# Second mixing output in eight units of three passes, with the block inversion and the first inverse's expansion placed earlier

## The chip, the cores and the metric

The kernel runs on one core of one Trainium2 chip. The metric is the device time of one execution in microseconds (us). The profile is one execution on that core; its times count from the first instruction.

## What is computed

Two transformer-like blocks run over 256 tokens of width 1024, all in float32. The first block (attention, an LRU mixer, two gated feed-forward layers) is not touched. The change lies in the second block, between its input projections and its feed-forward layer:

```python
p = concat([h_ctx, h_lat]) @ w_in               # q k v z, rq rk rv rg, for 512 tokens
o_gdn = rms_norm(o_f + o_b, gdn_norm_g) * silu(z)      # gated delta rule, forward and backward
o_ret = head_group_norm(r_f + r_b, ret_norm_g) * silu(rg)   # retention, forward and backward
y = concat([o_gdn, o_ret])                      # 256 latent tokens x 1024
x = x + g1 * (y @ w_out)                        # "second mixing output"
x = x + g2 * swiglu(modulate(rms_norm(x), sh2, sc2), w_ffn_in, w_ffn_out)
```

The delta rule needs, for each tile of 128 tokens, head and direction, the inverse of a unit triangular matrix. The kernel inverts its 16x16 diagonal blocks by substitution, row after row, for all tiles at once, and joins them to the 128x128 inverse in three levels of products.

## The kernel before

Each engine has its own program, written out by hand; semaphores order them. There is no scheduler. Weights stream from memory in chunks of 2 MB into `ring`, which has three slots; `stream_order` is the order of the chunks, and the load of chunk i waits on SyncE's queue until chunk i-3 is counted in `chunk_used`. The last chunks before the feed-forward layer are `win` (eight), `wo2` (two halves of w_out) and `ada` 9 to 11 (modulation), then `up2`.

**Split products.** Most products are made of two reduced-precision parts. For a unit of weights (128x1024) ScalarE copies the high part into `parts` (`high_parts`, L311; an input of the product as well, L334), VectorE subtracts it to get the low part (`low_parts`, L315 and L346), and TensorE makes three passes, low by high, high by high, high by low. `parts` holds three units, so unit n+3 can be copied only when TensorE has counted unit n in `parts_used`. `SplitProjection` does this for a product whose input is turned tiles: a unit is 12 matmuls of 512 columns; of the last three units it makes the first 128 tokens' rows first. `high_ahead` and `low_ahead` split a unit's weights before its input exists.

**The stretch in question**, in order:

- The projections end with `w_rq` and `w_rg` (four units each). `rotated` applies the rotary embedding to `w_rq`'s result on VectorE and `gated` the gate of `w_rg`.
- VectorE inverts the 16x16 blocks (`invert_rows`): row i is one multiply and one reduction for each direction, of i*i elements. Rows 1 to 8 come before `gated`, rows 9 to 11 in retention's step 0 and rows 12 to 15 in its step 1. The result goes through memory (`inverses_out`, then 16 small DMAs, `inverse_rows_in`), and `expand` spreads it over the tile `X`.
- Retention runs in four steps over both directions. In steps 0 to 2 TensorE makes the state's update (`rdS`) and VectorE adds it (`update_state`, L1771 and L1774); in steps 2 and 3 TensorE makes the scores (`rqk`), the product with the state and, after VectorE's mask (L1828), the product with the values (`ro`), which `output_part` evicts (L1757 to L1762).
- The delta rule runs in four steps. In each TensorE turns `X` (L2306), ScalarE copies it (`XT`), three levels of `Y` and `Z` products alternate with VectorE (L1891 to L1912), then come `wT`, `vnew`, the state's update and, in steps 2 and 3, `o`, evicted by `output_part` again. `beside` is a table of small VectorE tasks put beside these levels.
- Then `y` is turned tile by tile, and `heads_projection` multiplies it by w_out in full float32, from `ring` directly: retention's half first, the delta rule's half after its norm. One matmul of 128x512 in float32 stands in the trace as two records.
- `beside_norm` makes modulation chunks 10 and 11 beside the residual and the norm, and `up_ffn2` starts (L407).

`parts` lies over columns 13312 to 20991 of the scratch memory `arena`, so the tiles of retention and the delta rule that lie there exclude split weights.

## Time and profile before

| | |
|---|---|
| median of 3 runs | 1436.04 us (1434.91 to 1438.17) |
| the profiled execution's own time | 1437.29 us |
| its span, first to last instruction | 1435.5 us |
| TensorE busy | 1341.1 us, 93% |
| VectorE busy | 908.0 us, 63% |
| ScalarE busy | 673.0 us, 47% |
| mean granted TensorE clock | 0.968 |

The busy share is an average over all stages. The stretch of the change runs from about 1012 us (the end of VectorE's work for `w_rq`'s weights) to 1238 us (the first matmul of the feed-forward layer), 226 us; there TensorE does wait.

### The profile page before, as it was taken

How to read it: one execution, taken by the hardware profiler on the slowest of the kernel's cores; microseconds unless marked ns; L12 is line 12 of the kernel's file. 1: busy time of each engine (PE TensorE's matmuls, PEld its weight loads, DVE VectorE, ACT ScalarE, POOL GpSimd, SP SyncE). 2: the span in 40 equal slices, each digit the busy share in tenths (PEclk: the TensorE clock that was granted, in tenths of full speed). 3: DMA queues.
4: the chain of work that ended last, by engine and by line, in shares of the span. 5: the costliest groups of instructions: out<-in, count | busy, mean ns of one | idle time of the engine just before them, and what ended most of it. 6: DMA issues, size and time to landing. Idle time of an engine off the chain costs nothing.

```text
span 1435.5 us, 19067 instructions
## 1 busy us (share of the span) xinstructions
PE 1341.1 (93%) x7776; PEld 1141.9 (80%) x7776; DVE 908.0 (63%) x1394; ACT 673.0 (47%) x1043; POOL 65.5 (5%) x105
## 2 busy tenths in 40 slices
PE   7999999888999999899999989999879989899997
PEld 5899978777888878868888767868779884588885
DVE  4444443356888758577889767558776541566665
ACT  4444544345676645755666653334401110455453
POOL 1000000000000000000000000210121100000000
PEclk9999999998999999999999999999979998999999
DMA  9643334546454566356545472125410003554451
GB/s 361 252 175 120 118 135 159 208 152 240 162 191 176 184 226 250 116 196 241 195 177 183 177 271 93 59 86 186 159 16 1 1 1 117 222 189 176 176 196 69
DMA packets 31525, 230.16 MB, mean 160 GB/s; under 512 B 11168, under 2 KB 14624, under 8 KB 18512
## 3 DMA queue, kind: packets, MB, share of 16 engines
q1 hardware_dynamic: 25712, 218.27, 41.9%
q10 hardware_dynamic: 4720, 7.02, 1.3%
q0 software_dynamic: 1008, 3.67, 0.6%
q8 instruction: 61, 1.00, 0.3%
q14 instruction: 24, 0.20, 0.0%
HBM read 225.50 MB, written 3.44 MB: 159 GB/s over the span
## 4 chain that ended last, share of the span: by engine, by line
PE 80%; DVE 11%; ACT 5%; issue 2%; DMA 1%; POOL 0%; POOLq 0%; ACTq 0%; DVEq 0%; SPq 0%
PE ps L407 17%; PE ps L197 14%; PE ps L579 13%; PE ps L458 10%; PE ps L411 9%; PE ps L546 5%; PE ps L449 5%; PE ps L518 4%; DVE parts L315 2%; PE ps L490 2%; ACT parts L311 1%; DVE arena L1463 1%; ACT arena L1086 1%; DMA ring<-in_W 1%; PE ps L1987 1%
## 5 line engine op out<-in xcount | busy, mean ns | idle before, releaser
L315 DVE TENSOR_TENSOR parts<-ring,parts 128x1024 fp32r<-128x1024 f32 x346 | 422.7, 1226 | 290.9 <-ACT parts L311 222.9
L311 ACT ACTIVATE parts<-ring 128x1024 fp32r<-128x1024 f32 x346 | 365.1, 1057 | 303.6 <-PE ps L411 104.8
L407 PE MATMUL ps<-hall,parts 128*128 128x512 f32 x1120 | 397.9, 399 | 12.3 <-DVE hall L271 6.5
L411 PE MATMUL ps<-hall,parts 128*128 128x256 f32 x1120 | 316.2, 282 | 0.0
L407 PEld LDWEIGHTS ps<-hall,parts 128*128 128x128 f32 x1120 | 212.4, 190 | 64.5 <-issue 12.0
L579 PE MATMUL ps<-parts 128*128 128x512 f32 x1032 | 241.9, 394 | 8.5 <-DVE parts L346 7.5
L579 PEld LDWEIGHTS ps<-parts 128*128 128x128 f32 x1032 | 194.3, 190 | 53.7 <-DVE parts L346 12.3
L411 PEld LDWEIGHTS ps<-hall,parts 128*128 128x128 f32 x1120 | 214.3, 191 | 0.0
L197 PE MATMUL ps<-arena 128*128 128x128 f32 (+2 forms) x1238 | 171.9, 300 | 22.7 <-DMA arena<-in_rel_bias 7.3
L197 PEld LDWEIGHTS ps<-arena 128*128 128x128 f32 (+1 forms) x1238 | 160.5, 202 | 32.0 <-issue 8.6
L458 PE MATMUL ps<-hall,parts 128*128 128x256 f32 x1152 | 140.4, 284 | 0.7 <-ACT arena L1050 0.7
L458 PEld LDWEIGHTS ps<-hall,parts 128*128 128x128 f32 x1152 | 138.7, 192 | 1.1 <-ACT arena L1050 1.1
L1463 DVE SCALAR_TENSOR_TENSOR arena<-arena,par 128x255 f32<-128x255 f32 (+1 forms) x192 | 80.1, 480 | 18.8 <-ACT arena L1086 18.0
L546 PE MATMUL ps<-parts,hall 128*128 128x512 f32 x336 | 82.6, 402 | 2.1 <-DVE parts L315 2.1
L546 PEld LDWEIGHTS ps<-parts,hall 128*128 128x128 f32 x336 | 63.2, 190 | 17.9 <-DVE parts L315 3.0
L449 PE MATMUL ps<-parts,hall 128*128 128x512 f32 x288 | 68.6, 398 | 4.5 <-DVE hall L266 2.5
L449 PEld LDWEIGHTS ps<-parts,hall 128*128 128x128 f32 x288 | 54.7, 192 | 17.6 <-ACT arena L1050 3.3
L518 PE MATMUL ps<-hall,parts 128*128 128x512 f32 (+1 forms) x288 | 60.8, 374 | 5.2 <-issue 2.8
L518 PEld LDWEIGHTS ps<-hall,parts 128*128 128x128 f32 x288 | 50.5, 200 | 14.4 <-issue 5.8
L287 POOL TENSOR_SCALAR smallp<-small 128x1 f32<-128x1 f32 x24 | 5.5, 228 | 1056.7 <-ACT arena L629 646.2
L1086 ACT ACTIVATE arena<-arena,par 128x256 f32<-128x256 f32 x96 | 49.6, 587 | 4.0 <-DVE arena L390 4.0
L490 PE MATMUL ps<-hall,parts 128*128 128x256 f32 x384 | 47.4, 285 | 1.5 <-DVE hall L266 1.3
(216 smaller groups left out, 1095.2 us busy)
## 6 DMA issues: line engine op xcount, KB each, us to landing
ring<-in_W SPq DMA_DIRECT2D x100, 2048.0 KB, 8.3
arena<-distance_tables SPq DMA_DIRECT2D x8, 384.0 KB, 7.5
gains<-in_gains POOLq DMA_DIRECT2D x5, 512.0 KB, 7.4
ring<-in_W SPq DMA_DIRECT2D x4, 512.0 KB, 9.1
arena<-in_gate_w ACTq DMA_DIRECT2D x1, 2048.0 KB, 10.8
matrices<-arena ACTq DMA_DIRECT2D x8, 256.0 KB, 2.8
x<-in_x SPq DMA_DIRECT2D x1, 1024.0 KB, 6.3
gates<-in_ada_gate_b POOLq DMA_DIRECT2D x2, 512.0 KB, 6.4
```

What stands on the lines that cost most here:

```text
L197: return nc.tensor.matmul(o, l, r, start=start, stop=stop)
L311: return nc.scalar.activation(unit_weights(n, 0, weights), weights, ACT.Copy)
L315: return nc.vector.tensor_tensor(unit_weights(n, 1, weights), weights, unit_weights(n, 0, weights), ALU.subtract)
L407: last = nc.tensor.matmul(ps[:, b, :].rearrange("p (a b) -> p a b", a=2), w[:, 0, :], hparts[:, :, k, :], start=k == 0, stop=False)
L411: last = nc.tensor.matmul(ps[:, b, 0:S], w[:, 1, :], hparts[:, 0, k, :], start=False, stop=k == KT - 1)
L449: last = nc.tensor.matmul(ps[:, banks[t], :], hparts[:, x_part, k, t * P:(t + 1) * P], parts[:, u % NPARTS, w_part, w0:w0 + 512], start=k ...
L458: last = nc.tensor.matmul(ps[:, banks[n // 2], (n % 2) * S:(n % 2 + 1) * S], parts[:, u % NPARTS, w_part, k * P:(k + 1) * P], hparts[:, x_ ...
L490: last = nc.tensor.matmul(ps[:, 4 + 2 * (i % 2) + n // 2, (n % 2) * S:(n % 2 + 1) * S], parts[:, u % NPARTS, w_part, k * P:(k + 1) * P], h ...
L518: last = nc.tensor.matmul(o, parts[:, u % NPARTS, w_part, k * P:(k + 1) * P], h, start=k == 0 and x_part == 1, stop=k == KT - 1 and w_part ...
L546: last = nc.tensor.matmul(ps[:, b, :], hall[:, t // TT, x_part, k, t % TT * P:(t % TT + 1) * P], parts[:, u % NPARTS, w_part, w0:w0 + 512] ...
L579: last = nc.tensor.matmul(ps[:, 2 * t + half, :], parts[:, n % NPARTS, x_part, D + t * P:D + (t + 1) * P], parts[:, n % NPARTS, w_part, w0 ...
L1463: last = v.scalar_tensor_tensor(dst, src, pcol("ffn_conv_w", (layer * 3 + tap) * 48 + ft), dst, ALU.mult, ALU.add)
```

## The change

1. `invert_rows` moves. Rows 1 to 5 go ahead of the low part of `w_rg`'s first unit, rows 6 to 8 ahead of the second, rows 9 and 10 ahead of the third, and rows 11 to 15 behind the second rotation. Retention's loop holds none. `gated` goes ahead of the masks of retention's decay. The inversion's tile no longer shares memory with the rotation's scratch tile, which moves into `parts`' input columns, and `rotated` takes its operands as 2x2 heads.
2. `expand(0)` goes from behind retention into its last step, ahead of that step's evictions (it waits for the same DMAs), and TensorE turns `X` at the delta rule's step 0 without waiting for retention's outputs; its first `Y` product waits for them.
3. The second mixing output becomes `p_mix2`, a `SplitProjection` of eight units. Units 0 and 1 are split ahead, by ScalarE in the delta rule's step 2 and by VectorE in step 3; retention's half of `y` is turned and copied in step 3; unit 2 waits for the last `o`, since the delta rule's last tiles lie in its buffer. Modulation 9 goes ahead of unit 0, and its chunk ahead of `wo2` in the stream. Tiles of the delta rule leave `parts`' other two buffers for memory of finished operands (`kdec`, `St`, `ET`, `E`).

```diff
-            + [("win", i, 0) for i in WIN_ORDER] + [("wo2", 1, 0)] + ada[9:10] + [("wo2", 0, 0)] + ada[10:12]
+            + [("win", i, 0) for i in WIN_ORDER] + ada[9:10] + [("wo2", 1, 0), ("wo2", 0, 0)] + ada[10:12]
...
+        p_mix2 = SplitProjection(4, [("wo2", 1, 0), ("wo2", 0, 0)], region(2048, KT, S), KT, lambda e, kk: e.wait_ge(S_("yT_out"), kk // 2 + 1))
...
-        later_tiles = [region(16384 + 512 * i, H4, P) for i in range(9)]
-        rkdec, rPm, rSt, St = (later_tiles[2 * i:2 * i + 2] for i in range(4))
-        kdec, ET = rkdec, rPm
-        E = [later_tiles[8], tmpr]
+        later_tiles = [region(16384 + 512 * i, H4, P) for i in range(6)]
+        rkdec, rPm, rSt = (later_tiles[2 * i:2 * i + 2] for i in range(3))
+        kdec = [region(11264 + 512 * d, H4, P) for d in range(2)]
+        St = [kT[:, :, P * d:P * (d + 1)] for d in range(2)]
+        ET = [vT[:, :, P * d:P * (d + 1)] for d in range(2)]
+        E = rET
...
+                if step == 2:
+                    for ahead_unit in (0, 1):
+                        high_ahead(act, p_mix2.first + ahead_unit)
...
+                if step == STEPS - 1:
+                    y_out(0)
+                    y_out(1)
+                    high_parts(act, p_mix2.first + 2)
+            act.wait_ge(S_("o"), 4)
+            high_parts(act, p_mix2.first + 3)
+            ada_rows(ADA_MIDDLE)
             for i, t in enumerate((1, 0)):
                 act.wait_ge(S_("o_out"), 7 + i)
                 head_squares(0, t)
+            high_parts(act, p_mix2.first + 4)
+            for ahead_unit in (4, 5):
+                high_ahead(act, p_mix2.first + ahead_unit)
+            y_out(2)
+            y_out(3)
+            p_mix2.scalar(act)
...
+            invert_rows(1, 6)
+            low_parts(dve, u0 + 29)
+            invert_rows(6, 9)
+            low_parts(dve, u0 + 30)
+            invert_rows(9, 11)
             low_parts(dve, u0 + 31)
             w_rq.done(dve)
             rotated(w_rq, 0, rq[:, 0, :, :], 0)
             low_parts(dve, u0 + 32)
             rotated(w_rq, 1, rq[:, 1, :, :], TT2 + TT + 1)
+            invert_rows(11, BLK)
...
-                    if step == 0:
-                        invert_rows(9, 12)
-                    if step == 1:
-                        invert_rows(12, BLK)
+                if step == STEPS - 1:
+                    dve.wait_ge(S_("lvl_in"), 16)
+                    dve.wait_ge(S_("inverse_rows_in"), 16 * 2 * NB)
+                    for d in DIRS:
+                        expand(0, d)
...
-                      (2, 0): lambda: delta_gates(0), (2, 2): lambda: delta_gates(1)}
+                      (2, 0): lambda: delta_gates(0), (2, 2): lambda: delta_gates(1),
+                      (3, 0): lambda: low_ahead(dve, p_mix2.first), (3, 1): lambda: low_ahead(dve, p_mix2.first + 1)}
...
+                if step == STEPS - 1:
+                    low_parts(dve, p_mix2.first + 2)
                 if step >= 2:
                     for d in DIRS:
                         dve.wait_ge(S_("o"), later(step, d))
                         output_part(0, step, d, 4 * d, 4 * d + 2)
+            low_parts(dve, p_mix2.first + 3)
...
-            pe.wait_ge(S_("mixed"), 2)
             pe.wait_ge(S_("vnew_out"), 8)
-            y_transposes(4, 5)
-            y_transposes(6, 7)
-            pe.wait_ge(S_("yT_a"), 2)
+            ada(ADA_MIDDLE)
             pe.wait_ge(S_("o_out"), 8)
-            heads_projection(1)
-            ada(ADA_MIDDLE)
+            p_mix2.unit(pe, 0)
             ada_turn(ADA_MIDDLE)
+            for kk in range(1, 4):
+                p_mix2.unit(pe, kk)
             pe.wait_ge(S_("mixed"), 4)
             pe.wait_ge(S_("ada_out"), ADA_MIDDLE + 1)
-            y_transposes(0, 4)
-            y_transposes(2, 6)
-            pe.wait_ge(S_("yT_a"), 3)
-            pe.wait_ge(S_("yT_v"), 1)
-            heads_projection(0)
+            y_transposes(2)
+            y_transposes(3)
+            p_mix2.tensor(pe, 4)
```

VectorE's program from the last unit of `w_rg` on, before: a rotation's end (L1650), the inversion (products L1789 into `row`, reductions L1795), the masks (L1818), the gate (L1654) and retention's first two evictions (L1771).

```order
L1650 TENSOR_TENSOR arena<-arena 128x512
L1810 MEMSET arena 128x512
L1813 MEMSET arena 128x16 x2
...
L1789 TENSOR_TENSOR row<-arena,row 128x64 x2
L1795 TENSOR_REDUCE arena<-row 128x8 x2
L1818 TENSOR_TENSOR arena<-arena,cst 128x4x128 x2
L1654 SCALAR_TENSOR_TENSOR arena<-arena,ps 128x512 x2
L1771 COPY arena<-ps 128x512 x2
L1789 TENSOR_TENSOR row<-arena,row 128x81 x2
L1795 TENSOR_REDUCE arena<-row 128x9 x2
```

The same place of the change (rotation L1669, inversion L1766 and L1772, gate L1673, masks L1844, evictions L1824 and L1827):

```order
L1669 TENSOR_TENSOR arena<-arena 128x512
L1766 TENSOR_TENSOR row<-arena,row 128x121 x2
L1772 TENSOR_REDUCE arena<-row 128x11 x2
...
L1766 TENSOR_TENSOR row<-arena,row 128x225 x2
L1772 TENSOR_REDUCE arena<-row 128x15 x2
L1673 SCALAR_TENSOR_TENSOR arena<-arena,ps 128x512 x2
L1844 TENSOR_TENSOR arena<-arena,cst 128x4x128 x2
L1824 COPY arena<-ps 128x512 x2
L1827 SCALAR_TENSOR_TENSOR arena<-arena,ps 128x128 x8
```

Rows 1 to 10 now stand ahead of the second-last rotation, rows 11 to 15 behind the last, and nothing of the inversion between retention's evictions.

TensorE's program from the delta rule's last step to the norm, before (transposes of `y` L2370, the full float32 product L197 from `ring`, modulation L1987):

```order
L197 MATMUL ps<-row,arena 128x128 x8
L197 MATMUL ps<-arena 128x128 x40
L2370 MATMUL ps<-cst,arena 128x128 x8
L197 MATMUL ps<-ring,arena 128x512 x16
L1987 MATMUL ps<-ring,condT 32x512 x8
L197 MATMUL ps<-sel,row 128x2 x4
L2370 MATMUL ps<-cst,arena 128x128 x8
L197 MATMUL ps<-ring,arena 128x512 x16
L1987 MATMUL ps<-ring,condT 32x512 x16
```

And of the change (transposes L2317, split product L579, modulation L2014):

```order
L197 MATMUL ps<-row,arena 128x128 x8
L2317 MATMUL ps<-cst,arena 128x128 x8
L197 MATMUL ps<-arena 128x128 x40
L2014 MATMUL ps<-ring,condT 32x512 x8
L579 MATMUL ps<-parts 128x512 x12
L197 MATMUL ps<-sel,row 128x2 x4
L579 MATMUL ps<-parts 128x512 x36
L2317 MATMUL ps<-cst,arena 128x128 x8
L579 MATMUL ps<-parts 128x512 x48
```

Eight transposes went ahead of the last step's 40 products, and 32 float32 matmuls became 96 of one pass.

## Rows read from the trace of the kernel before

**Rows 1.** The page: busy time, share of the span and instructions of each engine.
```profile
PE 1341.1 (93%) x7776; PEld 1141.9 (80%) x7776; DVE 908.0 (63%) x1394; ACT 673.0 (47%) x1043; POOL 65.5 (5%) x105
```

**Rows 2.** Stretches: length, busy time (instructions) of each engine, granted clock, DMA.
```profile
1036.40:1045.00 8.60, 8.41 (x48) 8.25 (x48) 5.25 (x14) 0.00 (x0) 4.92 (x5) 0.65 0.01 2
1067.60:1090.00 22.40, 21.88 (x167) 21.30 (x168) 13.56 (x32) 4.83 (x20) 2.08 (x2) 0.88 0.00 1
```

**Rows 3.** Chain that ended last, retention: start, length, what.
```profile
1036.48 3.77 PE ps L197 x16
...
1040.96 0.71 DVE row L1789 x2
...
1053.27 0.61 DVE arena L1828
...
1066.91 0.61 DVE arena L1807
...
1069.60 3.63 PE ps L197 x16
```

**Rows 4.** VectorE alone in stretches: length, busy (instructions), granted clock, DMA.
```profile
1011.96:1026.32 14.36, 8.81 (x13) 1.00 0.41 147
1026.49:1033.64 7.15, 6.48 (x35) 1.00 0.70 246
1040.88:1043.91 3.03, 2.89 (x10) 0.75 0.02 5
1043.91:1045.23 1.32, 1.25 (x5) 1.00 0.00 0
1047.30:1053.27 5.97, 5.73 (x18) 0.95 0.00 0
```

**Rows 5.** VectorE in order of time; in brackets idle before, and its releaser.
```profile
1030.70 1.72 DVE L1789 TENSOR_TENSOR row<-arena,row 128x49 f32<-128x49 f32 x2
...
1035.10 1.29 DVE L1654 SCALAR_TENSOR_TENSOR arena<-arena,ps 128x512 f32<-128x512 f32 x2
```

**Rows 6.** GpSimd in order of time.
```profile
1030.32 2.04 POOL L959 TENSOR_TENSOR arena<-arena 128x512 f32<-128x512 f32 x2 [20.07 <-PE ps L546]
```

**Rows 7.** TensorE in order of time, the delta rule's end.
```profile
1180.45 1.04 PE L2370 MATMUL ps<-cst,arena 128*128 128x128 f32 x8
...
1204.07 1.05 PE L197 MATMUL ps<-sel,row 128*128 128x2 f32 x8 [0.72 <-ACT row L1025]
```

**Rows 8.** Chain that ended last, delta rule's last step to the feed-forward layer.
```profile
1160.42 19.31 PE ps L197 x168
...
1182.43 1.14 DVE arena L1762 x4
...
1185.88 15.61 PE ps L197 x32
...
1207.53 16.73 PE ps L197 x32
...
1224.42 8.89 DMA ring<-in_W
...
1238.22 0.76 PE ps L407
```

**Rows 9.** Chain that ended last, first block's second mixing output (eight units).
```profile
609.89 16.82 PE ps L579 x60
626.74 1.06 ACT parts L311
...
628.14 1.23 DVE parts L315
...
629.75 5.75 PE ps L579 x24
```

**Rows 10.** Chain that ended last, first block's end to the second's projections.
```profile
842.84 5.75 PE ps L579 x24
...
858.97 24.79 PE ps L518 x96
```

More of the change, by code:

```diff
@@ L1736, in _, with invert_rows @@
                 normalized("qn", t)
+            def invert_rows(first, end):
+                if first == 1:
+                    dve.wait_ge(S_("blocks_in"), 16 * 2 * NB)
+                for i in range(first, end):
+                    for d in DIRS:
+                        done = slice(BLK - i, BLK) if d else slice(0, i)
+                        r = BLK - 1 - i if d else i
+                        prod = block_tmp[:, d, 0:i * i].rearrange("p (c j) -> p c j", c=i)
+                        last = v.tensor_tensor(prod, inverses[:, d, done, done].rearrange("p j c -> p c j"),
+                                               blocks[:, d, r, done].unsqueeze(1).to_broadcast([P, i, i]), ALU.mult)
+                    link(last)
+                    for d in DIRS:
+                        done = slice(BLK - i, BLK) if d else slice(0, i)
+                        r = BLK - 1 - i if d else i
+                        last = v.tensor_reduce(inverses[:, d, r, done], block_tmp[:, d, 0:i * i].rearrange("p (c j) -> p c j", c=i),
+                                               AX.X, ALU.add, negate=True)
+                    if i < BLK - 1:
+                        link(last)
+                    else:
+                        last.then_inc(S_("inverses"), 1)
+            link(v.memset(inverses[:, :, :, :], 0.0))
+            for d in DIRS:
+                diagonal = inverses[:, d, :, :].rearrange("p i j -> p (i j)")[:, 0:BLK * BLK:BLK + 1]
+                last = v.memset(diagonal, 1.0)
+            link(last)
+            invert_rows(1, 6)
[3 more added lines that the diff above has]
+            invert_rows(9, 11)
             low_parts(dve, u0 + 31)
@@ L1807, in expand @@
                 v.tensor_tensor(X[d].rearrange("p h (b j) -> p h b j", b=NB), rows, mask, ALU.mult).then_inc(S_("X_in"), 1)
-            link(v.memset(inverses[:, :, :, :], 0.0))
-            for d in DIRS:
-                diagonal = inverses[:, d, :, :].rearrange("p i j -> p (i j)")[:, 0:BLK * BLK:BLK + 1]
-                last = v.memset(diagonal, 1.0)
-            link(last)
-            invert_rows(1, 9)
+            for i in range(TT):
+                gated(w_rg, i, rgt, TT2 + TT)
             for d in DIRS:
@@ L1818, in _ @@
                 link(v.tensor_tensor(rET[d], rET[d], bh(cst[:, C_GE if d else C_LE, :]), ALU.mult))
-            for i in range(TT):
-                gated(w_rg, i, rgt, TT2 + TT)
             for step in range(STEPS):
@@ L1878, in _ @@
                     dve.wait_ge(S_("Y_zero"), 3)
-                    dve.wait_ge(S_("lvl_in"), 16)
-                    dve.wait_ge(S_("inverse_rows_in"), 16 * 2 * NB)
-                    for d in DIRS:
-                        expand(step, d)
                 if step:
@@ L2295, in _, with y_transposes @@
                         heads(4 * d + 2, rPm[d], rv[:, TILE_OF[d][step], :, :]).then_inc(S_("ro"), 1)
+            def y_transposes(i):
+                kind, h = int(i < 2), 2 * (i % 2)
+                for n in range(2):
+                    for t in range(TT):
+                        last = nc.tensor.transpose(ps[:, Y_BANK[i], n * S + t * P:n * S + (t + 1) * P], y2[kind][:, t, h + n, :], ident)
+                last.then_inc(S_("yT"), 1)
             for step in range(STEPS):
-                pe.wait_ge(S_("o_out"), 4 + max(step - 2, 0) * 2)
+                if step > 2:
+                    pe.wait_ge(S_("o_out"), 4 + (step - 2) * 2)
                 if step:
@@ L2330, in _ @@
                         last.then_inc(S_("Z"), 1)
+                if step == STEPS - 1:
+                    pe.wait_ge(S_("mixed"), 2)
+                    for d in DIRS:
+                        pe.wait_ge(S_("decay"), 2 * TT2 + 2 + later(step, d))
+                        y_transposes(d)
                 if step:
```

87 lines of the change are left out of this document (26 added, 61 removed).

## The prediction

> **What bounds the kernel now.** I read the page's engine line first: TensorE is busy 93% of the span [rows 1], so a gain has to come from its idle stretches, from stretches at a low clock, or from less TensorE work. Then the chain of work that ended last, for 1000 to 1240 us, and the same stretch engine by engine. Three places stand out.
>
> Retention: from its first product at 1036.48 to the delta rule's first `Y` product at 1069.60 it takes 33.1 us [rows 3], with TensorE at a granted clock of 0.65 of full speed in the first 8.6 us [rows 2]. The chain there goes through VectorE: inversion rows from 1040.96, more of them until the mask at 1053.27, `expand` at 1066.91 [rows 3]. Rows 9 to 11 take 3.03 + 1.32 = 4.4 us and rows 12 to 15 take 5.97 us [rows 4].
>
> The mixing output: 15.61 and 16.73 us of TensorE [rows 8], 32.3 us for 64 records, about 0.49 us each half a matmul each.
>
> Behind it: the chain goes from TensorE to the DMA of the first feed-forward chunk (8.89 us), which waits for the slot of `wo2`'s second half, and the first matmul starts at 1238.22, 14.0 us after the product's end at 1224.26 [rows 8].
>
> **A, up to retention's start.** VectorE has 14.36 us between 1011.96 and 1026.32, of which 8.81 are busy [rows 4], so 5.5 us are free; the last rotation ends there. Into this go the memsets and rows 1 to 8, 7.15 us [rows 4], of which 1.3 us is one product pair of 1.72 us, whose neighbours in size take 0.34 and 0.43; GpSimd's products ran beside it from 1030.32 to 1032.36 [rows 5, 6]. Without that excess it is 5.8. Rows 9 and 10, 3.03 us [rows 4], at a low-cost reading 2.4. Together 8.2, less 5.5 free: the last rotation ends 2.7 us later, at 1029.0. Behind it rows 11 to 15, 1.32 + 5.97 = 7.3 us [rows 4], to 1036.3. But GpSimd's products still start when `w_rg` is done, near 1030.3, now beside rows 11 to 15; I add half of the 1.3 us seen once, 0.7. The gate takes 1.29 us [rows 5] and ends at 1038.3, against 1036.4: **+1.9 us**, from +1.2 (no collision) to +2.5 (as in the trace).
>
> The GPSIMD Engine Reference of the Trainium skill (section Specifications) says that GpSimd's memory interfaces are shared with VectorE and contended by VectorE instructions with two inputs in that memory. By this rule the products of rows 11 to 15, which have two such inputs, are slowed as the pair of 1.72 us was; that speaks against the change, by at most the +2.5 already in the range.
>
> The low parts of `w_rg`'s four units are done, by the same count, at about 1016.6, 1020.1, 1023.7 and 1026.9. `w_rg` ends where GpSimd's products are released, 1030.3 [rows 6], and a unit takes 2.8 to 2.9 us (half of 5.75, rows 9), so TensorE begins it near 1019 and needs them at 1019.0, 1021.8, 1024.6 and 1027.4. The margin falls from 2.4 to 0.5 us; cost nothing, and each us beyond it moves retention one us.
>
> **B, retention.** Time T counts from its first product. The first two products take 3.77 us at the low clock [rows 3], the next two to T = 6.1 (48 records in 8.41 us, rows 2, less the first 16, make 1.16 for each of four groups of 8). `update_state` follows, four instructions a direction like those of 1.14 us [rows 8], to 7.2. TensorE makes two scores and two products with the state at 0.92 each (19.31 us for 168 records, rows 8, 8 records a product) to 9.8, and two more updates to 11.6; VectorE adds them by 12.9 and evicts step 2 in 3.6 (twice a copy of 0.7 and such four instructions) by 16.5. Masks 1.3 to 17.8, `expand` 1.3 (twice the 0.61 from which the chain goes on) to 19.1, the last evictions 3.6 to 22.7. `X` has been turned and copied beside them, and the first `Y` product starts at about T = 22.8. Before it was 33.1 [rows 3]: **-10.3 us**. 7.6 of it is the inversion rows, less what TensorE now takes in their place; 2.7 is expansion, turning and copy (1066.91 to 1069.60). If half a us more is waited at each hand-over or the low clock lasts to the end, it is -7; if the low clock is shorter than before, -11.5. The inverses' way through memory took 13.6 us at most (the last row ended at 1053.27, and `expand` began at 1066.91 straight behind VectorE's own work, rows 3); from 1037 that is 1050.6, and it is needed at T = 17.8, 1056: hidden.
>
> **C, the delta rule.** In step 3, level 0, VectorE is on the chain into the products at 1160.42 [rows 8], and one unit's low part stands there now: 1.23 us, 1.13 from start to start [rows 9]. At level 1 it has TensorE's four products as cover and costs nothing. Eight transposes, 1.04 us [rows 7], join TensorE's unbroken 168 records. Before, they were hidden under VectorE's last evictions. The low parts of two inputs stand ahead of the last evictions and wait for ScalarE's two copies of `y`; by count they end at the last `o`: +0.1. Sum +2.3. Against that, the delta rule's first 22.4 us ran at a granted clock of 0.88 [rows 2], so a quarter of it at the lower level of 1.2 GHz, after an idle 3.7 us that becomes 1.5: I take back a third of the 2.7 us lost, 0.9. **+1.4 us**, from 0 to +3.
>
> **D, the mixing output.** The nearest rows are the same class in the first block: eight units from 609.89 to 635.50, 25.6 us, with one chain over ScalarE and VectorE of 3.0 us, from 626.74 to 629.75, nearly all beside TensorE's own work [rows 9]. The bare rate is 5.75 us for 24 matmuls, 0.24 each, 23 us for 96. To 25.6 I add modulation 9's turn 1.05 and eight transposes 1.04 [rows 7], and one wait: after the transposes come two copies of `y`, an input's high part and its low part (about 0.5 + 0.4 + 0.35 us beyond the transposes' own end), 1.4 us. That is 29.0 from the last eviction on. Before it was 1183.57 to 1224.26, 40.7 [rows 8], with 2.3 us ahead of it and 6.0 us between the halves. **-11.7 us**. Units 2 to 5 are split beside the squares and the norm, as their buffers come free; the norm's end (by this order about 10 us after the last eviction) lies ahead of unit 3's end (about 14). Bounds: at the bare rate 26, -14.5; with 1 us more of waiting for each of the last four units, -7.7.
>
> FP8 and Floating Point Precision of the Trainium skill (section TensorE Precision Notes) gives true float32 four passes. Three quarters of the 32.3 us would be 24.2 and the gain 1.2 us less than with 23 at the bare rate; The rows, 0.49 us a record and two records a matmul, against three times 0.24, say more; they decide.
>
> **E, behind it.** The slot is released at the first pass of unit 7, with 5 + 18 passes to go, 5.5 us before the end. The DMA of 8.9 us [rows 8] lands 3.4 us after the end, when ScalarE is still at its rows of modulation. What is left is the path without the DMA, as between the first block and the projections, which has the same two modulation chunks and shifted norm: 842.84 + 5.75 = 848.6 to 858.97, 10.4 us [rows 10]. **-3.6 us**, from -2 to -3.7. Nothing else of the feed-forward layer changes.
>
> **Sum.** +1.9 - 10.3 + 1.4 - 11.7 - 3.6 = -22.3 us, against the profiled execution's own 1437.3: 1415.0. That execution lay 1.25 above the median of the runs, so 1413.8, which I put at 1414. The forecast's own range is 1408 to 1420.
>
> **Rivals.**
>
> 1. VectorE is later than counted ahead of retention: a low part of `w_rg` comes late and the inversion collides more. For: margins of 0.5 us, and one pair took four times its size's time. Against: the free 5.5 us are measured. 4 to 6 us back: 1419. Chance 0.12.
> 2. The mixing output follows its buffers: unit n+3 waits for unit n, then 1.06 and 0.34 us of ScalarE, 1.23 and 0.38 of VectorE [rows 9], 3 us against 1.4 for a half unit at the end, and the clock drops in each wait. For: the wait in rows 9. Against: little of it was left on TensorE there, 25.6 us against 23. 4 waits of 1.5 us: 1420. Chance 0.08.
> 3. The gain is larger, since waits close and with them the low clock goes (0.65 and 0.88, rows 2): 1407. Chance 0.07.
> 4. The earlier inversion does nothing for retention, since the inverse's rows come late: VectorE then waits in `expand` ahead of the last evictions. It decides nothing below 5 us more than the 13.6 of before, and one for one beyond. With B gone: 1424. Against: nothing in the way grows. Chance 0.02.
> 5. Slower: TensorE's clock stays at the lower level through the mixing output and the first feed-forward units, since bursts of 2.8 us alternate with waits. 96 passes would take 22.5 us more, which alone gives 1436; two feed-forward units of about 2.8 us more each give 1442. It makes the kernel slower from 25 us of full-speed work at half speed on. For: 8.6 us at 0.65 and 22.4 at 0.88 [rows 2]. Against: 0.24 us a pass in rows 9, with such waits between. Chance 0.07, half of it over 1439.
>
> Forecast 0.64. The range 1407 to 1424 leaves out a part of rivals 3 and 5 and some of the bounds' ends. 0.2%, 2.9 us, is about what a measurement of this kernel can tell from no change: faster 0.93, within 0.03, slower 0.04.
>
> **What the changed profile would show.** Right: retention's first product near 1038.3; no inversion rows in its chain; first `Y` near 1061; step 3 of the delta rule 2 us longer; eight units within 29 us of the last eviction; the next matmul about 10.4 us after them with no DMA in the chain. Wrong: VectorE low parts as releasers of TensorE in `w_rg` (rival 1) or in units 4 to 7 (rival 2), VectorE released by a DMA in `expand` (rival 4), a granted clock near 0.5 over the mixing output (rival 5).

## The result, and the profile after

The changed kernel takes 1408.9 us, the median of 4 runs (1407.0 to 1410.6). The kernel before takes 1436.9 beside it (4 runs, 1434.9 to 1438.2). The ratio is 0.9818, with a 95% interval of 0.9802 to 0.9835: 26 us faster by the ratio, 28 by the two medians. The forecast was 1414, with a range of 1407 to 1424 and an own range of 1408 to 1420. Three single executions in all that follows (two of the kernel before, one of `slot_late`) took 2211 to 4402 us and are left out of every ratio.

The page of the changed kernel, engine lines, which answer to [rows 1]: TensorE has more instructions than before and is busy 20 us less.

```profile
PE 1321.2 (94%) x7808; PEld 1136.3 (81%) x7808; DVE 917.6 (65%) x1409; ACT 683.7 (49%) x1060; POOL 65.4 (5%) x105
```

The stretch of the change in the changed kernel, cut at the same places of the program. Columns as in [rows 2]: start and end, length; busy time and instructions of TensorE's matmuls, its weight loads, VectorE, ScalarE, GpSimd; granted clock; DMA.

```profile
1021.04:1039.91 18.87, 13.77 (x75) 11.62 (x74) 18.32 (x43) 5.83 (x11) 2.13 (x2) 0.92 0.49 187
1039.91:1062.44 22.53, 19.56 (x152) 19.00 (x153) 17.66 (x46) 1.08 (x2) 8.86 (x9) 0.91 0.14 17
1062.44:1099.05 36.61, 34.61 (x297) 33.47 (x297) 26.15 (x60) 4.73 (x20) 5.67 (x5) 1.00 0.01 2
1099.05:1140.55 41.50, 37.53 (x328) 37.00 (x329) 22.90 (x59) 8.95 (x14) 4.08 (x4) 1.00 0.00 1
1140.55:1174.11 33.56, 31.16 (x272) 29.21 (x272) 17.76 (x41) 8.66 (x19) 0.00 (x0) 1.00 0.02 5
1174.11:1200.41 26.30, 24.42 (x116) 19.68 (x120) 14.31 (x26) 10.79 (x28) 1.98 (x2) 1.00 0.59 207
1200.41:1210.26 9.85, 7.47 (x53) 3.36 (x53) 8.03 (x11) 7.22 (x14) 1.49 (x4) 1.00 0.89 336
```

Four of the same stretches of the kernel before, beside [rows 2], which cut them otherwise: retention, the delta rule's first and last step, and the mixing output.

```profile
1036.48:1069.60 33.12, 24.38 (x153) 23.54 (x154) 25.97 (x72) 0.60 (x1) 8.93 (x9) 0.76 0.11 17
1069.60:1107.79 38.19, 36.20 (x296) 35.06 (x296) 26.16 (x60) 5.32 (x21) 5.67 (x5) 0.95 0.01 2
...
1149.30:1183.57 34.27, 32.03 (x256) 31.46 (x256) 14.84 (x37) 6.06 (x16) 0.00 (x0) 0.92 0.00 1
1183.57:1224.26 40.69, 36.48 (x100) 16.06 (x104) 5.89 (x15) 4.58 (x14) 2.79 (x4) 0.87 0.27 104
```

The seven stretches after are, line by line, `w_rg`'s first pass up to retention, retention, the delta rule's first step, its second and third, its last, the mixing output, and what lies behind it up to the feed-forward layer's first matmul. The lengths before and after, by term:

| term of the prediction | before | after | difference | predicted |
|---|---|---|---|---|
| A, up to retention's start | 17.50 | 18.87 | +1.4 | +1.9 |
| B, retention | 33.12 | 22.53 | -10.6 | -10.3 |
| C, delta rule | 113.97 | 111.67 | -2.3 | +1.4 |
| D, mixing output | 40.69 | 26.30 | -14.4 | -11.7 |
| E, behind it | 13.96 | 9.85 | -4.1 | -3.6 |
| sum | 219.24 | 189.22 | -30.0 | -22.3 |

The stretch itself starts 2.1 us later in this execution (1021.04 against 1018.98), by a program that differs up to there in a few of VectorE's instructions and in the order of its last weight chunks; the inversion is not the cause, since TensorE runs into `w_rg`'s first pass without a wait in both. That, and 1.4 us less behind the stretch (197.28 against 195.84), make the difference of the two spans, -29.4.

The chain of work that ended last in the changed kernel, mixing output (start, length, what):

```profile
1172.97 1.14 DVE arena L1815 x4
1174.16 3.02 PE ps L579 x12
1177.17 0.79 PE ps L197 x8
1177.96 8.28 PE ps L579 x36
1186.24 0.45 PE ps L2317 x4
1186.71 1.09 ACT arena L1339 x2
1187.80 0.31 ACT parts L334
1188.13 0.44 DVE parts L346
1188.62 3.03 PE ps L579 x12
1191.67 1.06 ACT parts L311
...
1193.07 1.23 DVE parts L315
...
1194.68 5.73 PE ps L579 x24
1200.41 3.57 PE ps L2014 x32
```

It answers to [rows 8]. The first unit starts 0.05 us after the last `o` (VectorE's L1815 ends at 1174.11), and four units run with only modulation 9's turn between them. Turning `y` and splitting it take 2.38 us (1186.24 to 1188.62, counted as 2.44). Then the chain leaves TensorE for 3.0 us, over a unit's high and low part, as in [rows 9]; TensorE works beside it and is idle 0.33 us. No DMA stands in the chain any more.

### The profile page after: what moved, and what is told of

Same layout as the page of the kernel before. It is cut to its first block, busy times and chain, and to the rows that moved or that the text cites. A ratio compares the mean times of both kernels' runs of the same rounds, so it can differ in the third digit from the quotient of the medians.

```text
span 1406.1 us, 19176 instructions
## 1 busy us (share of the span) xinstructions
PE 1321.2 (94%) x7808; PEld 1136.3 (81%) x7808; DVE 917.6 (65%) x1409; ACT 683.7 (49%) x1060; POOL 65.4 (5%) x105
## 4 chain that ended last, share of the span: by engine, by line
PE 80%; DVE 12%; ACT 5%; issue 2%; DMA 0%; POOL 0%; ACTq 0%; POOLq 0%; DVEq 0%
PE ps L407 17%; PE ps L579 14%; PE ps L197 11%; PE ps L458 10%; PE ps L411 9%; PE ps L546 5%; PE ps L449 5%; PE ps L518 4%; DVE parts L315 3%; PE ps L490 2%; ACT parts L311 1%; DVE arena L1479 1%; PE ps L2014 1%; ACT arena L1087 1%; DVE arena L1815 1%
## 5 line engine op out<-in xcount | busy, mean ns | idle before, releaser
L315 DVE TENSOR_TENSOR parts<-ring,parts 128x1024 fp32r<-128x1024 f32 x354 | 432.5, 1226 | 286.5 <-ACT parts L311 216.5
L311 ACT ACTIVATE parts<-ring 128x1024 fp32r<-128x1024 f32 x354 | 373.5, 1057 | 308.1 <-PE ps L411 105.5
L579 PE MATMUL ps<-parts 128*128 128x512 f32 x1128 | 263.9, 393 | 12.2 <-DVE parts L346 10.0
L579 PEld LDWEIGHTS ps<-parts 128*128 128x128 f32 x1128 | 211.1, 189 | 62.5 <-DVE parts L346 15.8
L197 PE MATMUL ps<-arena 128*128 128x128 f32 (+2 forms) x1238 | 166.4, 294 | 22.9 <-DMA arena<-in_rel_bias 7.1
L197 PEld LDWEIGHTS ps<-arena 128*128 128x128 f32 (+1 forms) x1238 | 154.8, 196 | 32.2 <-issue 13.1
L1479 DVE SCALAR_TENSOR_TENSOR arena<-arena,par 128x255 f32<-128x255 f32 (+1 forms) x192 | 80.0, 480 | 18.7 <-ACT arena L1087 17.9
```

The lines of the kernel that those rows point to most:

```text
L197: return nc.tensor.matmul(o, l, r, start=start, stop=stop)
L311: return nc.scalar.activation(unit_weights(n, 0, weights), weights, ACT.Copy)
L315: return nc.vector.tensor_tensor(unit_weights(n, 1, weights), weights, unit_weights(n, 0, weights), ALU.subtract)
L579: last = nc.tensor.matmul(ps[:, 2 * t + half, :], parts[:, n % NPARTS, x_part, D + t * P:D + (t + 1) * P], parts[:, n % NPARTS, w_part, w0 ...
L1479: last = v.scalar_tensor_tensor(dst, src, pcol("ffn_conv_w", (layer * 3 + tap) * 48 + ft), dst, ALU.mult, ALU.add)
```

## The experiments

All were compared with runs of the kernel before on the same chip; ratios are to it, with a 95% interval, and a difference in us is the difference of two ratios times 1435. They were run in three sets, each on a chip of its own: `inv_only`, `mix_only`, `expand_back` and `before_filled`; `early_f32`, `slot_late`, `gate_first` and `best`; `after_again`, `after_filled` and `early_between`. The change's own 0.9818 is a measurement apart. The same program, run again as `after_again` in the third set, gave 0.9785, 4.7 us less, so a timed difference of under 5 us between sets, or to the change's 0.9818, shows nothing by itself; where it matters, the stretches of the profile decide.

### The two halves of the change apart

`inv_only` is the kernel before with the first two items of the change: `invert_rows` and `gated` moved, `expand(0)` in retention's last step. The mixing output is in float32 from `ring`, as before.

```diff
+            invert_rows(1, 6)
+            low_parts(dve, u0 + 29)
+            invert_rows(6, 9)
...
-                    if step == 0:
-                        invert_rows(9, 12)
-                    if step == 1:
-                        invert_rows(12, BLK)
+                if step == STEPS - 1:
...
+                        expand(0, d)
```

> The kernel before with only the inversion and the first expansion moved, the mixing output still in full float32. Theory (the parts add up): A and B are -9.2 us in the changed profile (+1.4 and -10.6), and about -2 more come with the clock of the delta rule's first step, so 9 to 12 us under before, about 1426; first product of retention to first Y product 22 to 23 us; from the last eviction to the mixing output's end 40 to 41 us as before. Rival (the better clock of the delta rule and of the mixing output belongs to the split product): the delta rule from first Y to last eviction stays at 114 us, and the gain is 8 to 9 us.

`mix_only` is the change with that part put back: `invert_rows`, `gated`, `expand(0)` and the turn of `X` stand as before, the mixing output is in eight units.

> The changed kernel with the inversion rows and the first expansion back at their places of before. Theory: retention takes 33 us again, mixing output 26 to 29 us, 9.9 to 10.4 us behind it; 16 to 19 us under before, about 1419; together with the other part the sum is the change's 28 us. Rival: the two parts need each other (fewer idle stretches, so a full clock into the mixing output), and the mixing output alone takes 28 to 30 us, 13 to 15 us under before.

Measured: `inv_only` 0.9931 (0.9906 to 0.9956), -9.9 us; `mix_only` 0.9898 (0.9881 to 0.9915), -14.6 us. The product of the two is 0.9830, inside the change's interval of 0.9802 to 0.9835 and above that of `after_again` (0.9764 to 0.9806). The stretches of `inv_only`, retention, the start of the delta rule's last step, and the mixing output:

```profile
1034.62:1056.87 22.25, 19.32 (x153) 18.76 (x153) 17.64 (x46) 1.09 (x2) 8.87 (x9) 0.92 0.14 17
1134.96:1146.10 11.14, 10.98 (x72) 10.80 (x73) 4.11 (x11) 2.39 (x4) 0.00 (x0) 0.74 0.01 1
1169.20:1209.93 40.73, 36.47 (x100) 16.02 (x104) 5.94 (x16) 4.58 (x14) 2.79 (x4) 0.87 0.26 104
```

And of `mix_only`, retention, the mixing output, and what is behind it:

```profile
1029.51:1062.57 33.06, 24.37 (x153) 23.52 (x153) 26.03 (x72) 0.60 (x1) 8.93 (x9) 0.76 0.11 17
1178.75:1205.05 26.30, 24.42 (x116) 19.67 (x120) 14.31 (x26) 10.84 (x28) 2.17 (x3) 1.00 0.58 208
1205.05:1214.91 9.86, 7.48 (x53) 3.37 (x53) 8.03 (x11) 7.16 (x13) 1.30 (x3) 1.00 0.89 334
```

Each stretch is that of the changed kernel where its half of the change is in (22.25 and 26.30), and that of before where it isn't (33.06 and 40.73), to 0.3 us. So B and D with E are separate: nothing of the earlier inversion is needed for the faster mixing output, or the other way round. `inv_only` also has the delta rule's first step at 36.6 us and a clock of 1.00, against 38.2 at 0.95: that gain belongs to the first half of the change. From `w_rg`'s first pass to the feed-forward layer `inv_only` takes 207.95 us and `mix_only` 202.90, 11.3 and 16.3 less than the 219.24 of before; the timed 9.9 and 14.6 us (12.1 to 17.1) agree with that within their intervals. The two make 27.6 of the 30.0 us in the changed kernel's profile. What is missing is the full clock at the start of the delta rule's last step, which neither half has (11.14 and 12.31 us there) and that profile has (9.53).

### `expand(0)` alone

`expand_back` is the change with `expand(0)` and the turn of `X` behind retention's last evictions again, and the inversion early.

```diff
-                if step == STEPS - 1:
...
-                        expand(0, d)
...
+                    for d in DIRS:
+                        expand(step, d)
...
-                if step > 2:
-                    pe.wait_ge(S_("o_out"), 4 + (step - 2) * 2)
+                pe.wait_ge(S_("o_out"), 4 + max(step - 2, 0) * 2)
```

> The changed kernel with the first expansion and the turn of X behind retention's last evictions again, everything else as changed. Theory of the prediction: 2.7 us slower than the changed kernel, and 3.5 to 4.5 if TensorE's longer idle stretch brings the low clock back into the delta rule's first step, 1411.5 to 1413. Rival: ScalarE or GpSimd set the first Y product, and the time stays within 1 us of the changed kernel's.

Measured: 0.9846 (0.9825 to 0.9868), 4.0 us more than the change, though the intervals overlap and the sets differ, so the time alone shows nothing. Its retention and the delta rule's first step:

```profile
1041.23:1066.36 25.13, 20.93 (x152) 20.38 (x153) 17.64 (x46) 0.60 (x1) 8.82 (x9) 0.84 0.13 15
1066.36:1104.79 38.43, 36.59 (x297) 35.57 (x296) 26.19 (x60) 5.33 (x21) 5.67 (x5) 0.94 0.01 1
```

Retention is 2.6 us longer than with the change, the 2.7 that the prediction counted for expansion, turning and copy. The first step is 1.8 us longer with the same instructions: TensorE is idle 3.69 us ahead of it here, 2.32 us with the change, and the granted clock is 0.94 against 1.00. The placement is worth 4.4 us in the profile, 1.8 of it by the clock of the first step, and some of the 2.6 is clock too: the turn of `X`, eight records, takes TensorE 1.94 us there and 1.04 with the change.

### What made the mixing output so much shorter

The prediction compared 32.3 us of float32 with 96 passes of 0.24. `early_f32` is `inv_only` with all of the mixing output's order but without three passes: retention's half of `y` is turned and copied in the delta rule's last step, modulation 9 goes ahead of the product, and the product is still in float32 from `ring`.

```diff
+                    for d in DIRS:
+                        pe.wait_ge(S_("decay"), 2 * TT2 + 2 + later(step, d))
+                        y_transposes(4 + 2 * d, 4 * d + 3)
...
-            y_transposes(4, 5)
-            y_transposes(6, 7)
+            ada(ADA_MIDDLE)
```

> The kernel with the inversion and expansion moved, whose mixing output is still in full float32, but retention's half of y is turned and copied in the delta rule's last step and modulation 9 made ahead of the product, as in the change. Theory (most of D and E is the three passes, the clock they keep, and the slot released earlier): from the last eviction to the product's end 35 to 37 us instead of 40.7, the last step 0.9 us longer, 14 us behind it; about 3 to 4 us under the kernel with the inversion alone, about 1419. Rival (the gain is the earlier turning, which lets the product start with the last eviction): 10 us or more under it, near 1413.

`early_between` is that kernel with modulation 9 between the two halves, where it was.

> The kernel with the mixing output in full float32 and y turned early, with modulation 9 put back between the two halves (its weights of 32 columns in TensorE ahead of the second half, and TensorE idle ahead of the first). Theory (what ran just ahead sets the clock of each half): the first half takes 15.6 us instead of 13.97 and the second 16.5 to 16.7 instead of 13.97, and with the modulation between them the stretch from last eviction to the product's end is 37.5 to 38.5 us instead of 31.0. Rival (the early turning alone gives the clock): both halves stay at 13.97 and the stretch takes 33 us.

Measured: `early_f32` 0.9892 (0.9873 to 0.9910), `early_between` 0.9906 (0.9890 to 0.9922). The mixing output of `early_f32` (the stretch), and then TensorE in order of time, the two halves; in brackets idle before and its releaser:

```profile
1174.04:1205.07 31.03, 29.80 (x84) 13.97 (x88) 6.04 (x15) 3.60 (x17) 2.84 (x4) 1.00 0.36 132
```

```profile
1174.10 13.97 PE L197 MATMUL ps<-ring,arena 128*128 128x512 f32 x32 [1.19 <-issue]
1191.10 13.97 PE L197 MATMUL ps<-ring,arena 128*128 128x512 f32 x32 [0.83 <-ACT arena L1340]
```

TensorE in `early_between`:

```profile
1172.96 15.67 PE L197 MATMUL ps<-ring,arena 128*128 128x512 f32 x32 [3.21 <-DVE arena L1806]
1188.56 1.92 PE L1999 MATMUL ps<-ring,condT 128*32 128x512 f32 x16
1194.50 17.00 PE L197 MATMUL ps<-ring,arena 128*128 128x512 f32 x32 [0.83 <-ACT arena L1340]
```

I had expected 35 to 37 us of `early_f32`; it took 31.0, and that miss settles the question. A float32 half takes 13.97 us at the full clock (0.44 a record). The 15.61 and 16.73 of before [rows 8] therefore held 4.4 us of lower clock. `early_between` shows both again, 15.67 behind 3.2 us of idle TensorE and 17.00 in the half that comes after the norm's wait, at 38.8 us from the last eviction to the end; its rival, both halves at 13.97, did not happen. So the gain of 14.4 us is made up thus: 40.7 to 31.0 comes with the product still in float32, by turning earlier and filling with modulation 9: 4.4 us of clock, 3.0 of waits (TensorE idle 4.2 us before, 1.2 here), 1.9 of modulation 9's passes, which now run in the wait ahead of the last eviction, and 0.4 of small pieces; 31.0 to 26.3 is what three passes give, 4.7 us. The time follows only in part: `early_f32` is 5.6 us under `inv_only` (3 to 4 expected, 10 by its rival, and the sets differ), where their stretches up to the feed-forward layer differ by 8.6 (199.34 against 207.95), and 10.6 us over the change, of which 8.5 is in the two stretches, the 4.7 and 3.8 behind the product, where the chunk's slot comes free only at its end (13.65 us against 9.85).

### The slot of `wo2`'s second half

`slot_late` is the change with that slot counted free at the last pass but one of the last unit, where it was at the unit's first pass.

```diff
-                        if frees:
+                        if frees or (frees_late and w_part == 1 and half == 0):
...
+                late = self.number == 4
```

> The changed kernel with the slot of the second half of w_out released at the last pass but one instead of at the first pass of the last unit, 5.4 us later. Theory (E is the DMA off the path): the DMA of 8.9 us lands 8.9 us behind the product's end, ScalarE's two high parts follow, and the first feed-forward matmul starts 13.5 to 14 us behind it instead of 9.85; 3.5 to 4.5 us slower than the changed kernel, about 1413. Rival (E is the clock or the evictions): 9.9 us as in the changed kernel and the same time.

Measured: 0.9847 (0.9824 to 0.9870), 4.1 us more than the change; the intervals overlap here too, and the profile has to decide. The chain of `slot_late`:

```profile
1195.80 5.52 PE ps L579 x23
...
1201.48 8.15 DMA ring<-in_W
1209.65 2.00 ACT parts L311 x2
1211.66 0.92 ACT hall L256 x2
```

The DMA is back in the chain, as in [rows 8], and the feed-forward layer's first matmul comes 13.0 us after the product's end instead of 9.85. The expectation was 13.5 to 14. The release of one slot 5.5 us earlier is worth 3.2 us of E's 4.1. The other 1.0 lies in the DMA, which took 8.15 us here and 8.89 in the kernel before, and in the slot, free one pass (0.24 us) before the product's end here and behind it there.

### Lower clock, filled from before and from after

The prediction's rival 3 says that closing waits brings clock. `before_filled` keeps every wait of the kernel before and gives TensorE matmuls that nobody reads while it waits: three float32 matmuls of 512 columns ahead of the delta rule's first turn, three ahead of its last step, four ahead of the mixing output.

```diff
+                if step == 0:
+                    pe.wait_ge(S_("rPm"), 4)
+                    filler(0, 3)
...
+                if step == 3:
+                    filler(1, 3)
...
+            filler(1, 4)
```

> The kernel before with matmuls that nobody reads in three idle stretches of TensorE: three of 512 columns in float32 ahead of the delta rule's first turn, three ahead of its last step, four ahead of the mixing output. Theory (what I under-sized is the clock, which follows idle stretches): granted clock near 1.0 in the delta rule's first and last step and in the first half of the mixing output, 3 to 7 us under before, about 1431. Rival (the changed kernel's clock was better by chance of the execution, or the fillers lie in the way): same time as before within 1.5 us, or slower.

Measured: 0.9966 (0.9954 to 0.9977), -4.9 us with more work and no wait removed. Its delta rule's first step from the turn of `X` on, the start of the last step, the first and the second half of the mixing output:

```profile
1066.95:1104.88 37.93, 35.80 (x304) 34.30 (x304) 26.58 (x61) 5.87 (x22) 5.67 (x5) 1.00 0.01 2
1146.38:1154.77 8.39, 8.24 (x72) 8.05 (x72) 4.11 (x11) 2.28 (x4) 0.00 (x0) 1.00 0.01 2
1180.23:1194.16 13.93, 13.93 (x32) 6.00 (x32) 1.37 (x5) 0.00 (x0) 0.31 (x1) 1.00 0.00 0
1200.52:1216.91 16.39, 16.39 (x33) 6.91 (x33) 2.45 (x2) 1.15 (x2) 0.75 (x2) 0.85 0.32 138
```

The start of the last step is 8.39 us at a granted clock of 1.00 where the kernel before and `inv_only` take 11.1 at 0.74; the first step from the turn of `X` takes 37.93 against 40.14 (1067.65 to 1107.79) in the kernel before; the first half of the product is 13.93 against 15.61, and the second, which has no such matmuls ahead of it, still takes 16.39 at 0.85. This is rival 3 shown by itself.

The same was tried on the changed kernel: `after_filled` (five such matmuls ahead of retention, three ahead of the last step, two ahead of the feed-forward layer), beside `after_again`, the changed kernel unaltered.

> The changed kernel with matmuls that nobody reads in three idle stretches of TensorE: five of 512 columns in float32 ahead of retention, three ahead of the delta rule's last step, two ahead of the feed-forward layer. Theory (each idle stretch brings a low clock that costs 1.5 to 3 us): 4 to 6 us under the changed kernel in the same set. Rival (the clock moves elsewhere in the kernel by as much, or waits take it up, as with the gate first): within 2 us of it.

> The changed kernel, unaltered, beside the two below. Theory (the full clock in the delta rule's last step was the luck of one execution; the mixing output's belongs to the change): the profile shows that step's first stretch (the turn of X to the first product behind level 0) at 12.3 us with the low clock, not 9.5, and the mixing output at 26.3 us and a granted clock of 1.00 again. Rival: 9.5 us again. The ratio to before again 0.980 to 0.984.

Measured: `after_filled` 0.9813 (0.9799 to 0.9828), `after_again` 0.9785 (0.9764 to 0.9806). In `after_filled` retention took 20.9 us instead of 22.5 and the start of the last step 9.53; in `after_again` that start was at a lower clock:

```profile
1139.65:1150.52 10.87, 9.58 (x72) 9.39 (x72) 5.25 (x12) 2.39 (x4) 0.00 (x0) 0.87 0.01 2
1174.55:1200.91 26.36, 24.48 (x116) 19.67 (x120) 14.31 (x26) 10.78 (x28) 1.98 (x2) 1.00 0.58 206
```

Up to the feed-forward layer `after_filled` takes 187.6 us, 1.6 and 3.0 less than the two profiles of the changed kernel (189.2 and 190.6); this does not show in the time, which is not shorter than `after_again`'s. The second line is D again, the same to 0.06 us as in the first profile. The first tells that C's -2.3 us was lucky in part: this start stood at 1.00 in the changed kernel's first profile, and at 0.74 to 0.87 in its second, in the kernel before and in six of the seven experiments without fillers. The seventh, `early_between`, had it at 1.00 and 8.39 us. Ahead of it TensorE was idle for 3.09 us in each of them.

### The gate earlier still

Retention waits 7.7 us after `w_rg`'s end, for VectorE. `gate_first` moves the inversion's rows 14 and 15 behind the gate, and the masks of retention's decay behind step 1's updates. `best` is that kernel with two, three and two matmuls that nobody reads, as in `after_filled`.

```diff
-            invert_rows(11, BLK)
+            invert_rows(11, 14)
...
-            for d in DIRS:
-                dve.wait_ge(S_("decay"), 2 * TT2 + d + 1)
-                link(v.tensor_tensor(rET[d], rET[d], bh(cst[:, C_GE if d else C_LE, :]), ALU.mult))
+            invert_rows(14, BLK)
```

> The changed kernel with the gate of w_rg ahead of inversion rows 14 and 15 and the masks of retention's decay behind step 1's updates. Theory (A is VectorE being late for retention's first product): TensorE starts retention about 3.3 us earlier, rows 14 and 15 lie beside its first products, and about 3 us of it stay: 1406. Rival (the wait is for ScalarE's evictions, or rows 14 and 15 delay the first state as much as the gate was early): within 1 us of the changed kernel.

> The kernel with the gate first, and with matmuls that nobody reads in three idle stretches of TensorE: two ahead of retention, three ahead of the delta rule's last step, two ahead of the feed-forward layer. Theory (the low clock behind each idle stretch costs 1.5 to 3 us): granted clock near 1.0 in all three, 4 to 6 us under the kernel with the gate first alone, about 1401. Rival (the fillers do not keep the clock there, or lie in the way): same time as the gate first alone.

Measured: `gate_first` 0.9827 (0.9803 to 0.9851), `best` 0.9823 (0.9805 to 0.9842): no gain over the change's 0.9818. TensorE in `gate_first`, and one product of the inversion on VectorE:

```profile
1039.66 3.19 PE L197 MATMUL ps<-arena 128*128 128x128 f32 x16 [1.93 <-ACT arena L1234]
...
1044.21 13.23 PE L197 MATMUL ps<-arena 128*128 128x128 f32 x104 [1.37 <-DVE arena L1824]
```

```profile
1041.04 1.71 DVE L1766 TENSOR_TENSOR row<-arena,row 128x225 f32<-128x225 f32 x2
```

Retention starts 4.6 us after `w_rg`'s end, 3.2 us earlier. But the rows that were moved are still to be made, now inside retention, where the matmuls wait for VectorE's evictions; row 15's products, the line above, take 1.71 us beside one of GpSimd's, where the change needs 0.97. The first `Y` product comes 1.3 us earlier only, and the delta rule's first 96 records then take 13.0 us, at a granted clock of 0.85 in the first 11, where the change's take 11.4 at 1.00. The gain moved downstream and was lost there. In `best` the start of the last step was at 1.00 (9.53 us) as expected, but the delta rule's first records were at 0.85 again, and the expected 4 to 6 us did not come.

## Why the prediction was right, and where it was off

**What bounds the kernel.** Right. All three places were bounds: retention mended alone (`inv_only`) and the mixing output with what is behind it (`mix_only`) gave time, and the slot put back alone (`slot_late`) brought its wait back.

**A, +1.9, measured +1.4.** The count of VectorE's free time held: `w_rg`'s low parts were done at 1018.9, 1022.4, 1025.5 and 1028.6, within 0.4 us of the count if the 2.1 us by which this execution is later are added, and its 48 passes took 11.15 us with no wait for one, so rival 1 did not happen. The collision with GpSimd did, on one row. VectorE, and GpSimd's product that ran beside it:

```profile
1031.76 0.71 DVE L1766 TENSOR_TENSOR row<-arena,row 128x144 f32<-128x144 f32 x2
1032.50 0.51 DVE L1772 TENSOR_REDUCE arena<-row 128x12 f32<-128x144 f32 x2
1033.05 1.68 DVE L1766 TENSOR_TENSOR row<-arena,row 128x169 f32<-128x169 f32 x2
...
1035.36 0.88 DVE L1766 TENSOR_TENSOR row<-arena,row 128x196 f32<-128x196 f32 x2
```

```profile
1032.36 2.13 POOL L960 TENSOR_TENSOR arena<-arena 128x512 f32<-128x512 f32 x2 [19.78 <-PE ps L546]
```

Row 13's pair took 1.68 us while GpSimd worked; rows 12 and 14 took 0.71 and 0.88. That is about 0.9 us for the one pair that began beside it, like the 1.3 in [rows 5], and not a slowing of every row from 11 on; the reduction at 1032.50, with one input, took 0.51. The Trainium skill's GPSIMD Engine Reference (section Specifications), which says that VectorE instructions with two inputs in the shared memory contend with GpSimd, agrees with this pair and this reduction.

**B, -10.3, measured -10.6.** Right by its own steps: the chain has step 2's evictions done at T = 16.3, the masks at 17.5, `expand` at 18.7 and the first `Y` product at 22.5, counted at 16.5, 17.8, 19.1 and 22.8. In the chain no inversion row is left, `expand` ran at 1057.38, ahead of the last evictions, released by VectorE's own work and not by a DMA (rival 4 did not happen). `expand_back` gives 2.6 us for its share of the 10.3, which was counted as 2.7. The clock has a part in B as well: TensorE was busy 24.4 us of retention before, at 0.76, and 19.6 after, at 0.91, with the same instructions. How much of the 10.6 that is, no run separates; `after_filled`, with matmuls ahead of retention, has it at 1.00 and in 20.9 us.

**C, +1.4, measured -2.3.** The added work is there, eight transposes and the low part: +2.0 us in the last step, counted as +2.3, and `mix_only`, which has it without the better clock, took 116.2 us for the delta rule, +2.2. The step that failed is the clock: I took back a third of the lost 2.7 us in the first step, 0.9, and it came back by 1.6 of 38.2 (behind a pause of 2.32 us, counted as 1.5); and I gave the last step no clock at all. Its first stretch in the kernel before:

```profile
1149.30:1160.42 11.12, 10.96 (x72) 10.77 (x73) 4.12 (x11) 2.39 (x4) 0.00 (x0) 0.74 0.01 1
```

`before_filled` takes 8.39 us at 1.00 there, 2.7 less. Together +2.0, -1.6 and -2.7 are the -2.3. But the last of these was luck in part: in the changed kernel's first profile this stretch was at the full clock, in its second it was not, and the delta rule took 113.0 us there, -1.0 against before.

**D, -11.7, measured -14.4.** The mechanism was right, and the term mis-sized is the base, 25.6 us for eight units [rows 9]. The granted clock of that stretch in the kernel before:

```profile
609.89:626.71 16.82, 16.82 (x61) 13.41 (x62) 16.40 (x24) 8.50 (x13) 0.00 (x0) 0.83 0.27 93
```

Sixty passes took 16.82 us there at 0.83, where 0.24 each make 14.4. In the changed kernel the clock is 1.00 and the 96 passes take 22.8 us (3.02 + 8.28 in the chain, then 24 in 5.73 twice, in TensorE's order of time), with 0.33 of waiting: 2.5 us less than the base, which is the miss but for 0.2. The bound of 26 us "at the bare rate" had foreseen it. The larger mistake is one of cause: I read 0.49 us a record as the cost of float32. It is 0.44 at the full clock; the rest was clock, which with the waits and the moved modulation 9 makes two thirds of the gain. Of four passes for true float32, which the Trainium skill states in FP8 and Floating Point Precision (section TensorE Precision Notes), three would be 0.75; the rows give 23 against 27.9 us at the full clock, 0.82, and they decide.

**E, -3.6, measured -4.1.** Right, and `slot_late` shows the cause of 3.2 of it.

**Rivals.** 1, 2, 4 and 5 did not happen: over the mixing output the granted clock was 1.00, and TensorE waited for VectorE 0.33 us between its last units. Rival 3, to which I gave 0.07, is most of the excess over the forecast. Of the 7.7 us by which the five terms exceed -22.3, 3.4 of C's 3.7 and 2.4 of D's 2.7 lie where the granted clock was higher than in the rows that I had priced from. I had that clock in [rows 2], and took some of it back in one term alone.

**How near to the edge.** All five terms were off to the same side. The measured 1408.9 lies nearer to rival 3's 1407 than to the forecast's 1414, and 1.9 us inside the range; the same program measured again (`after_again`) has a median of 1406.9, just outside it. That the range held owes something to luck.

**What stays open.** Why the same stretch, after the same idle time, runs at the full clock in one execution and below it in another. How much of B is clock. And whether the lower clock's price in the changed kernel, 1.6 to 3.0 us in the profiles, can be had in the time.

## What to carry to other kernels

Before pricing a rewrite of a matmul, ask for its time at the full clock: compare the mean of one in a stretch with granted clock 1.00 with the one to be replaced, and give the difference to the waits ahead of it; here 5.3 us of waits and moved work and 4.4 of clock were to be had without any change of the arithmetic. Matmuls that nobody reads, put into a wait, show in the profile what the clock costs there; whether the time follows is a second question (-4.9 us on the kernel before, nothing on the changed one). A stage moved ahead of another is worth it only where the engine that makes it has free time at the new place; where the work stays between the same two waits, as in `gate_first`, its gain is lost within microseconds.

## What the hardware showed beyond expectation

- A granted clock below 1.00 reached into the stage behind a wait: 16 float32 matmuls of 512 columns took 13.97 us at the full clock, 15.6 to 15.7 behind 3.2 to 4.4 us of idle TensorE, and 16.4 to 17.0 in the half behind some 6 us of waits and short instructions.
- The delta rule's first step began at the lower clock behind 3.69 us of idle TensorE (the kernel before, `mix_only`, `expand_back`) and at the full one behind 2.32 us in the changed kernel, twice, and in `inv_only`, `early_f32`, `early_between` and `slot_late`; in `gate_first` and `best`, where the work ahead of it differed, it ran low behind 2.32 us too (0.85 over its first 11 us).
- Single runs of one program scatter by several us (`after_again` from 1400.1 to 1407.5), and the same program gave ratios 4.7 us apart in two measurements. `w_rg`'s first pass started anywhere from 1012 to 1024 us in profiles of kernels that differ little up to there; the granted clock of the stages before has a part in it, and the rest was not followed. Differences below 5 us were not to be told apart by the time; in a stretch of the trace they were.
